# Hybrid decoder layer on 8 cores: guards of borrowed buffers split by pool, a bounded DMA backlog in the plan, and a final tile on attention's PSUM banks

## The reference, cut to what matters

```python
h = rms_norm(x, g_pre)
qa, ka, va, za, qb, kb, vb, zb, lr, gate_a, gate_b = split(h @ w_in)   # 1024 x 5648
oa = diff_attention(qa, ka, va, lam, slopes)          # 4 heads, two softmax maps, ALiBi, causal
ya = (rms_norm(oa, g_sub_a) * (1 - lam_init) * silu(za)) @ w_up_a      # 512 x 1024
ob = gla_chunked(qb, kb, vb, log_sigmoid(lr @ w_alpha + b_alpha) / 16)
yb = (rms_norm(ob, g_sub_b) * silu(zb)) @ w_up_b                       # 512 x 1024
y = sigmoid(gate_a) * ya + sigmoid(gate_b) * yb
return x + rms_norm(y @ w_out, g_post)
```

## Time and profile before

| | us |
|---|---|
| median of 3 runs | 1318.84 (1316.91 to 1324.17) |
| profiled execution, its own time | 1318.94 |
| span of its slowest core (core 4) | 1317.3 |
| spans of all cores | 1307.8 to 1317.3 |

### The profile page before, as it was taken

The page is one execution under the profiler, slowest core; times in us unless marked ns, Lnnn a source line. Parts: engine busy times, 40 slices in busy tenths (PEclk is TensorE's granted clock), DMA queues, the critical chain, the costliest instruction groups (busy, mean ns, idle before and its releaser), DMA issues.

```text
span 1317.3 us, 27507 instructions; the slowest of 8 cores (1307.8 to 1317.3 us)
## 1 busy us (share of the span) xinstructions
PE 1217.8 (92%) x9379; PEld 662.4 (50%) x9551; DVE 737.6 (56%) x2228; ACT 746.6 (57%) x1066; POOL 193.6 (15%) x307
## 2 busy tenths in 40 slices
PE   5898899699999999999999999999999999999986
PEld 2445345345555454555555555555555555555532
DVE  4769777734667447563475534755346553474344
ACT  3656445254754457555666556775568668666511
POOL 1213001300222002110121101211012010021000
PEclk9899999899999999999999999999999999999988
DMA  8896799754593438543484333744327441343441
GB/s 242 272 308 203 228 285 296 194 189 146 166 266 103 135 136 232 163 141 134 137 240 129 113 129 137 240 130 113 129 105 208 157 117 66 136 138 105 145 176 67
DMA packets 115618, 222.40 MB, mean 169 GB/s; under 512 B 68176, under 2 KB 76816, under 8 KB 100496
## 3 DMA queue, kind: packets, MB, share of 16 engines
q1 hardware_dynamic: 115472, 220.54, 54.5%
HBM read 173.06 MB, written 32.51 MB: 156 GB/s over the span
## 4 chain that ended last, share of the span: by engine, by line
PE 82%; DVE 5%; DMA 5%; issue 4%; SPq 2%; ACT 1%; POOL 0%; DVEq 0%; POOLq 0%; ACTq 0%
PE ps_pg L528 59%; PE ps_acc L528 14%; PE ps_qk L974 8%; DMA sb_wbuf<-wsc 2%; DMA sb_KT<-w_in 1%; SPq L501 1%; DMA sb_xr<-x 1%; SPq L606 1%; DVE sb_otmp L1015 1%; DMA sb_KT<-w_up_a 0%; DVE sb_ste L907 0%; ACT sb_PT L981 0%; DVE sb_szB L705 0%; PE ps_pg L532 0%; DVE sb_tmp L1142 0%
## 5 line engine op out<-in xcount | busy, mean ns | idle before, releaser
L981 ACT ACTIVATE sb_PT<-ps_qk 128x1024 bf16<-128x1024 f32 (+2 forms) x445 | 411.9, 970 | 188.1 <-PE ps_qk L974 182.1
L528 PE MATMUL ps_pg<-sb_hT,sb_wbuf 128*128 128x512 bf16 x1542 | 406.5, 382 | 11.3 <-DMA sb_wbuf<-wsc 3.1
L528 PE MATMUL ps_acc<-sb_V,sb_PT 128*128 128x129 bf16 x3340 | 373.1, 220 | 6.9 <-ACT sb_PT L981 1.8
L528 PEld LDWEIGHTS ps_acc<-sb_V,sb_PT 128*128 128x128 bf16 x3340 | 259.4, 98 | 114.9 <-issue 17.1
L528 PE MATMUL ps_pg<-sb_wbuf,sb_hT 128*128 128x512 bf16 x851 | 226.0, 383 | 7.8 <-issue 2.4
L528 PEld LDWEIGHTS ps_pg<-sb_hT,sb_wbuf 128*128 128x128 bf16 x1616 | 149.2, 98 | 155.6 <-issue 28.5
L1087 DVE SCALAR_TENSOR_TENSOR sb_tmp<-sb_tmp,ps_pg 128x512 f32<-128x512 f32 x120 | 82.2, 686 | 200.1 <-PE ps_acc L528 136.5
L1063 ACT ACTIVATE sb_tmp<-ps_pg 128x512 f32<-128x512 f32 x120 | 71.7, 597 | 119.8 <-PE ps_pg L528 68.1
L974 PE MATMUL ps_qk<-sb_QT,sb_KT 64*128 64x256 bf16 (+1 forms) x1754 | 130.3, 267 | 5.6 <-ACT sb_PT L981 2.2
L528 PEld LDWEIGHTS ps_pg<-sb_wbuf,sb_hT 128*128 128x128 bf16 x896 | 82.1, 98 | 86.8 <-issue 20.8
L1026 POOL TENSOR_TENSOR sb_statE<-sb_statE,sb_mhalf 128x1 f32<-128x1 f32 x128 | 73.2, 580 | 316.4 <-DVE sb_statE L1024 303.6
(11 more groups left out here) (170 smaller groups left out, 1257.5 us busy)
## 6 DMA issues: line engine op xcount, KB each, us to landing
sb_wbuf<-wsc SPq DMA_DIRECT2D x97, 1024.0 KB, 6.0
sb_KT<-w_in SPq DMA_DIRECT2D x88, 256.0 KB, 7.6
sb_xr<-x SPq DMA_DIRECT2D x34, 512.0 KB, 6.1
sb_xa<-x SPq DMA_DIRECT2D x30, 512.0 KB, 7.3
out<-sb_xr SPq DMA_DIRECT2D x30, 512.0 KB, 4.8
wsc<-sb_wbuf SPq DMA_DIRECT2D x10, 1024.0 KB, 9.9
wsc<-sb_V SPq DMA_DIRECT2D x5, 1024.0 KB, 11.4
sb_KT<-w_out SPq DMA_DIRECT2D x16, 256.0 KB, 8.9
```

Of the source, the lines that this page charges most:

```text
L528: return P.op(_pe(n), lambda e: e.matmul(out=out_f(), lhsT=lf(), rhs=rf(), start=start, stop=stop, **kw), reads=reads, writes=writes, mode ...
L981: P.op({"act": (0.075 + width / 600.0, 0.1)}, lambda e: e.activation(out=PT[pt.i][:, :, 0:width], in_=qk[:, 2 * half:2 * half + 2, 0:width ...
```

## The change

Three edits in the planner's rules, four in the program:

```diff
+BACKLOG = 3.0
+EARLY = {"w": "vxdone", "xa": "xrdone", "hb": "ytdone"}
...
-            self.readers.setdefault("vxdone", []).append(o)
-            self.readers.setdefault("xrdone", []).append(o)
-            self.readers.setdefault("ytdone", []).append(o)
+        if self.early_key is not None:
+            for p in {b.pool for b in [...] if isinstance(b, _Buf)}:
+                if p in EARLY:
+                    self.readers.setdefault(EARLY[p], []).append(o)
...
                     st = o.ready if o.ready > ef else ef
+                    if o.is_dma and st < dma_free - BACKLOG:
+                        st = dma_free - BACKLOG
...
-            def body(e):
-                for o in my_ops:
+            def body(e, finish=False):
+                for o in my_ops[-1:] if finish else my_ops[:-1] if eng_name == "sp" else my_ops:
...
-  ... accum_out=statB[st.i][:, hd:hd + 1]), reads=[f"cum{oi}"], writes=[(st, hd)])
+  ... accum_out=statB[st.i][:, hd:hd + 1]), reads=[f"cum{oi}"], writes=[(st, hd), f"junkd{hd}"])
...
-                        b = P.buf("pg")
+                        if t == ntiles - 1 and a >= 2:
+                            b, src = f"qk{a - 2}", lambda a=a: qk[:, 2 * (a - 2), :].bitcast(BF16).rearrange(...)
+                        else:
+                            b = P.buf("pg")
+                            src = lambda b=b: ptr(b)
...
-                    b = P.buf("pg")
+                    b = P.buf("pg") if t < ntiles - 1 or ntiles == 1 else f"acc{ab}"
...
+            def end_f(t, wo):
+                rows = []
+                for s in range(4):
...
+                    if s < 2:
+                        homes = [(lambda j=j: qk[:, j, :], f"qk{j // 2}") for j in (2 * s, 2 * s + 1)]
+                    elif s == 2:
+                        homes = [(lambda j=j: acc[j][:, :], f"acc{j}") for j in range(2)]
+                    else:
+                        bs = [P.buf("pg") for _ in range(2)]
+                        homes = [(lambda b=b: pg[b.i][:, :], b) for b in bs]
...
+                def part(s, kcs):
+                    for hh in range(2):
+                        out_f, key = rows[s][5][hh]
+                        for kc in kcs:
+                            mm(out_f, ..., kc == 0, kc == 7, 512, [f"yT{kc}"] + (...), [key])
+                def close(s):
...
+                        P.op({"act": (0.571, 0.2)}, ... func=AF.Square, scale=1.0 / 32.0, accum_out=statF[st.i][:, hh:hh + 1]) ...
...
+                    P.op({"dve": _dve(1)}, ... scalar_tensor_tensor(out=statF[:, 3:4], in0=statF[:, 0:1], scalar=EPS,
+                                                 in1=statF[:, 1:2], op0=ALU.add, op1=ALU.add) ...
...
+                        if s == 3:
+                            P.op({"sp": (0.38, 0.0)}, ... e.dma_start(out=out[g * 128:(g + 1) * 128, hh * 512:(hh + 1) * 512], ...
+                for s in range(2):
+                    part(s, range(7))
+                for s in range(2):
+                    part(s, range(7, 8))
+                    close(s)
+                for s in range(2, 4):
+                    part(s, range(8))
+                    close(s)
...
+                if last:
+                    end_f(t, wo)
+                    return
...
                 far = e.value_load(flag[0:1, 0:1])
                 with e.If(far != 0):
+                    if name == "sp":
+                        quick[name](e, True)
...
+                if name == "sp":
+                    quick[name](e, True)
```

More of the change, by code:

```diff
@@ L128, in op @@
         o.bufs = []
-        if self.early_key is not None and any(
-                isinstance(b, _Buf) and b.pool in ("w", "xa", "hb") for b in [k[0] if isinstance(k, tuple) else k for k in list(reads) + list(writes)]):
-            self.readers.setdefault("vxdone", []).append(o)
-            self.readers.setdefault("xrdone", []).append(o)
-            self.readers.setdefault("ytdone", []).append(o)
+        if self.early_key is not None:
+            for p in {b.pool for b in [k[0] if isinstance(k, tuple) else k for k in list(reads) + list(writes)] if isinstance(b, _Buf)}:
+                if p in EARLY:
+                    self.readers.setdefault(EARLY[p], []).append(o)
         for k in list(reads) + list(writes) + list(claim):
@@ L1112, in stage_e @@
                         ups(t, j, wu)
+            def end_f(t, wo):
+                rows = []
+                for s in range(4):
+                    g = 4 * t + s
+                    kind = "xa" if s >= 2 else "xr"
+                    xb, st = P.buf(kind), P.buf("statF")
+                    xt = lambda xb=xb, kind=kind: (xa if kind == "xa" else xr)[xb.i]
+                    load(lambda xt=xt: xt()[:], x[g * 128:(g + 1) * 128, :], lambda xb=xb, kind=kind: f"{kind}{xb.i}", [xb], 524288)
+                    if s < 2:
[5 more added lines that the diff above has]
+                        homes = [(lambda b=b: pg[b.i][:, :], b) for b in bs]
+                    rows.append((g, xb, st, xt, kind, homes))
+                def part(s, kcs):
+                    for hh in range(2):
+                        out_f, key = rows[s][5][hh]
+                        for kc in kcs:
+                            mm(out_f, lambda kc=kc, s=s: yT[:, kc, :][:, s * 128:(s + 1) * 128],
+                               lambda kc=kc, hh=hh: wo[kc // 4][0][:, (kc % 4) * 1024 + hh * 512:(kc % 4) * 1024 + (hh + 1) * 512], kc == 0, kc == 7, 512,
+                               [f"yT{kc}"] + ([f"wo{kc // 4}"] if kc % 4 == 0 else []), [key])
+                def close(s):
+                    g, xb, st, xt, kind, homes = rows[s]
+                    zs = []
+                    for hh in range(2):
+                        src, key = homes[hh]
+                        z = P.buf("tmp")
+                        zs.append(z)
+                        P.op({"act": (0.571, 0.2)}, lambda e, src=src, st=st, hh=hh: e.activation(out=junk[:, hh, :], in_=src(), func=AF.Square, scale=1.0 / 32.0,
+                                                                                              accum_out=statF[st.i][:, hh:hh + 1]),
+                             reads=[key], writes=[(st, hh), f"junk{hh}"])
+                        P.op({"dve": _dve(512)}, lambda e, src=src, z=z, hh=hh: e.tensor_tensor(out=tmp[z.i][:], in0=src(), in1=gpost[:, hh * 512:(hh + 1) * 512],
+                                                                                           op=ALU.mult), reads=[key, "gpost", (st, hh)], writes=[z])
+                    P.op({"dve": _dve(1)}, lambda e, st=st: e.scalar_tensor_tensor(out=statF[st.i][:, 3:4], in0=statF[st.i][:, 0:1], scalar=EPS,
+                                                                                 in1=statF[st.i][:, 1:2], op0=ALU.add, op1=ALU.add),
+                         reads=[(st, 0), (st, 1)], writes=[(st, 3)])
+                    P.op({"pool": (0.45, 0.1)}, lambda e, st=st: e.tensor_tensor(out=statF[st.i][:, 4:5], in0=statF[st.i][:, 3:4], in1=mhalf[:, 0:1], op=ALU.pow),
+                         reads=[(st, 3), "mhalf"], writes=[(st, 4)])
+                    for hh in range(2):
+                        P.op({"dve": _dve(512, 1.0, 1)}, lambda e, hh=hh, xt=xt, st=st, z=zs[hh]: e.scalar_tensor_tensor(
+                            out=xt()[:, hh * 512:(hh + 1) * 512], in0=tmp[z.i][:], scalar=statF[st.i][:, 4:5], in1=xt()[:, hh * 512:(hh + 1) * 512],
+                            op0=ALU.mult, op1=ALU.add), reads=[zs[hh], (st, 4), xb], writes=[(xb, hh)])
+                        if s == 3:
+                            P.op({"sp": (0.38, 0.0)}, lambda e, xt=xt, g=g, hh=hh: e.dma_start(out=out[g * 128:(g + 1) * 128, hh * 512:(hh + 1) * 512],
+                                                                                        in_=xt()[:, hh * 512:(hh + 1) * 512]),
+                                 reads=[xb, (xb, hh)], writes=[f"out{g}_{hh}"], dma=lambda hh=hh: f"sy{hh}", nbytes=262144)
+                    if s < 3:
+                        P.op({"sp": (0.38, 0.0)}, lambda e, xt=xt, g=g: e.dma_start(out=out[g * 128:(g + 1) * 128, :], in_=xt()[:]),
+                             reads=[xb, (xb, 0), (xb, 1)], writes=[f"out{g}"], dma=lambda xb=xb, kind=kind: f"s{kind}{xb.i}", nbytes=524288)
+                for s in range(2):
[6 more added lines that the diff above has]
+                    close(s)
@@ L1203, in program @@
                     stage_batt(t + 1, [])
-            P.op({"sp": (0.05, 0.0)}, lambda e: None, reads=[f"out{g}" for g in range(4 * ntiles)] + [f"wsc{c}" for c in range(NCHUNK)], writes=["end"])
+            P.op({"sp": (0.05, 0.0)}, lambda e: None, reads=[f"out{g}" for g in range(4 * ntiles)] + [f"out{4 * ntiles - 1}_{hh}" for hh in range(2)] + [f"wsc{c}" for c in range(NCHUNK)], writes=["end"])
             P.schedule()
@@ L1229, in body @@
                     full[name](e)
+                    if name == "sp":
+                        full[name](e, True)
+                if name == "sp":
```

(1 more changed line is left out.)

14 lines of the change are left out of this document (8 added, 6 removed).

## The result

| | before | after |
|---|---|---|
| median of 5 runs | 1319.23 us | 1302.04 us |
| ratio, 95% interval | | 0.9864 (0.9841 to 0.9888) |
| median span of the eight cores | 1312.0 | 1295.3 |

A forecast was written before the change was run, and what follows sets the result against it. PE was taken as the bound, busy 1217.8 of 1317.3 us, with its holes in the opening and at the end: 1318.94 - 2.9 - 0.5 - 2.0 - 0.7 - 2.0 - 4.5 + 1.0 = 1307.3 us, range 1296 to 1317.

The forecast's parts named there:

- Guards, -4.5: Opening: `xr` loads no longer wait behind weight stores, shrinking PE's hole; 4.5 us saved, between 3.9 and 9.7.
- the limit, 0: Planner's backlog limit: only re-makes the order of DMAs; counted zero, with 4 us to either side.
- The middle: Middle of the kernel: little to gain from the re-made order of DMAs.
- Flag load, -2.9: Kernel end: SP's flag load and branch run beside the last store's landing; 2.9 us saved, between 0.5 and 3.0.
- the sign asked for 0.5: Kernel end, sign of being right: SP's drain comes within 0.5 us of the last store's landing.
- The norm, -0.5: Last block: one folded operation lets POOL start 0.3 earlier and line 1151 follow sooner; 0.5 us saved, between 0 and 0.65.
- Stage F, -2.7: Last tile: early matmuls cover the wait for the last `yT`, 2.0 us, and waits for two banks go, 0.7.
- the weight chunk, -2.0: Last tile: early matmuls of F fill PE's wait for a weight chunk; 2.0 us saved, between 0 and 2.8.
- Attention's banks, +1.0: Last tile: `ups` groups now wait for attention's last evacuation; 1.0 us lost, at worst 3.4, at best no cost.
- The split store, 0: Kernel end: half of the last store issues 0.7 us earlier, but its landing is already beside the branch; counted nothing.
- SP behind stores: Slower rival, chance 0.11: late stores to `wsc` make SP and the loads behind it wait; 25.5 us added, 1332.8.
- everything fills: Faster rival, chance 0.11: opening and weight holes go whole, no loss at the banks; 1300.1, or 1296 with lucky order.

The follow-up runs named there:

- e3: The kernel before with only the guards changed to go by pool, nothing else: ratio 0.9980 (0.9959 to 1.0002) to the kernel before.
- e12: The changed kernel with the 3 us backlog limit holding only for the stores to `wsc`: 1312.72 us, ratio 0.9920 to the kernel before.
- e2: The changed kernel with the backlog limit so large that it never binds: ratio 0.9943 (0.9911 to 0.9975) to the kernel before.
- e4: The changed kernel with SP's last wait ahead of its flag load again: ratio 0.9889 (0.9866 to 0.9911) to the kernel before.
- e6: The changed kernel with the old stage F in the last tile: ratio 0.9886 (0.9864 to 0.9907) to the kernel before.
- e5: The changed kernel with the last tile's `ups` groups and turns in `pg` again: two runs, 1297.4 and 1299.6 us.
- e7: The changed kernel with the last block stored whole instead of in halves: ratio 0.9854 (0.9837 to 0.9872) to the kernel before.

## Why the prediction was right, and where it was not

The sign and the range held, and the places named did lose their holes. But several terms were sized wrong, the largest for a reason that the sum did not have, and some of these errors cancel.

- **Guards, -4.5, and the limit, 0: this step failed.** The opening gave 7.7 us of idle time, but the guards have no price of their own: alone they are worth 3.4 there and give 1.7 back in the middle (9.5 to 11.2), which e3 measured as no change. The prediction had the right next bound, DVE, and took its load as fixed ("that work stays"). The work stayed; its time did not. DVE was late because it converted w_out late, and the limit, treated as a re-made order without a sign, put the 1 MB stores behind the loads of w_out, which brought the conversions 13 us forward (e12). About half of these 13 us is the earlier landing of the loads; the other half is DVE's re-made list.
- **The middle.** "There is little to gain": 2.4 us of idle time went between 330 and 700 us (9.5 to 7.1), by the limit (e2), and not by its hold on the stores alone (e12). With the opening this makes 10.1 of the 10.5 by which attention ends earlier.
- **Flag load, -2.9.** Measured 2.7 (e4). The upper end was nearly right: SP's drain itself takes 0.06 or 0.013 us and comes 2.4 to 2.8 after the branch in e4, where nothing else is left to wait for. The Trainium skill, "Runtime: NRT & Kernel Launch", section "Instruction fetch mechanics", on a taken branch out of the fetched pages, is borne out by the trace as far as it goes: the time goes with the branch, beside the landing as well as behind it. Of SP's 3.0, 2.3 to 2.5 show in the end of the whole kernel: the sum had the branch's time end 0.3 ahead of the landing, but it ends 0.35 to 0.66 behind it and sets the end itself (the drain follows the landing by 0.8 on core 7, where the sign asked for 0.5).
- **The norm, -0.5.** Nothing: from the last matmul to DVE's last operation 4.03 before, 4.06 after. POOL did start early (1292.96), but block 2's second residual half stands ahead of block 3's two on DVE (one row of three at 1293.34): an engine's list in order gives back what one of its inputs gains.
- **Stage F, -2.7, and the weight chunk, -2.0.** e6 gives 4.0 for the new stage F, which holds the wait of 2.0 to 2.2 and the bank waits. The weight wait is gone too, but not by the step given: it stays away with the old stage F. The re-made order removed it; which move did it was not tried. It was also smaller than core 4 shows: before, it was 0.4 to 2.4 us on six cores (0.65 on core 0, which the prediction took to be free of it) and did not show on cores 1 and 7, and the lower clock behind it stood on cores 2 and 4 alone. Of the last tile's 3.8, the 4.0 and the 2.6 lost at the banks leave 2.4 to which no run gives a cause.
- **Attention's banks, +1.0.** Measured 2.6 (e5; 2.0 with the 0.6 that e5 gives back behind it): the mechanism and the place were right (2.85 at 1246.95), but the cover was thinner than taken. About 1.5 of the 2.6 is idle time; the rest goes with the lower granted clock behind the hole, which the term did not have.
- **The split store, 0:** confirmed by e7, and by the reason given: its landing lies beside the branch. **SP behind stores:** SP's waits rose from 6.1 to 23.6 us, above the 20 that the text named as a sign of trouble, with no cost seen on PE, which idles less there and on that core has no hole over 1.28 from 200 to 270 us. That mark was a bad one: a queue's waits count only by what stands behind them.

Against the core medians, then: up to the end of attention -10.5, last tile -3.8, end -2.5: the -16.7 measured, within the rounding. That 1307.3 came within 5 us of 1302.0 is in part luck: stage F gave 1.3 more than taken and attention's banks cost 1.6 more. The result lies nearer to the rival "everything fills" (1300.1), but not by its terms, since the banks were not free.

## What to carry to other kernels

Before crediting the removal of a wait, ask why the engine that is next is late, and whether another edit of the same change moves that cause: two edits may take off little alone (3.4 and 1.8 us of idle time here) and 7.7 together. Where a plan orders one shared DMA queue, large stores that nobody needs soon belong behind the loads that feed conversions, and here a limit that let the planner compare more DMAs by due time did this (with 3 us, not with 10). Test each part alone and each part missing; only both show an interaction.

## What the runs showed of the hardware

- Every engine pays for skipping the long program: in the changed kernel (core 7) PE's weight queue shows 3.77 us for its branch, and ACT's and POOL's drains come 3.1 and 3.0 after theirs. Only SP's, 2.5 to 2.8, was in the path of the kernel before.
- SP's flag load took 0.47 us behind the landing (e4; 0.47 or 0.48 before) and, right behind the issue of the last stores, 0.67 to 0.93 over the cores of the changed kernel, but only 0.48 to 0.51 in e7.
- Two stores of 256 KB, issued one behind the other, landed no sooner after their issue (3.8 us) than one of 512 KB (3.4; 3.50 to 3.75 for the last block in e7).
